# Two weight slots loaded and split ahead on GpSimd, and the last two rows' scale moved there

## What is computed

```
merged = sigmoid(mg_a + b_gate[0]) * y_a + sigmoid(mg_b + b_gate[1]) * y_b
sub = merged @ w_out                         # (512 x 2048) by (2048 x 2048)
z = ALPHA * x + sub
out = (z - mean(z)) * rsqrt(var(z) + eps) * ln_g + ln_b     # per row
```

## Time and profile before

| what | us |
|---|---|
| median of three runs | 1378.58 |
| the profiled execution | 1378.59 |
| its span | 1376.8 |
| TensorE busy | 1359.2 (99%) |
| TensorE's weight loads busy | 1153.8 (84%) |
| GpSimd busy | 683.3 (50%) |
| ScalarE busy | 575.9 (42%) |
| vector engine busy | 482.2 (35%) |
| TensorE's last product starts | 1365.86 |

### The profile page before, as it was taken

The page is one execution under the profiler, slowest core; times in us unless marked ns, Lnnn a source line. Parts: engine busy times, 40 slices in busy tenths (PEclk is TensorE's granted clock), DMA queues, the critical chain, the costliest instruction groups (busy, mean ns, idle before and its releaser), DMA issues.

```text
span 1376.8 us, 19878 instructions
## 1 busy us (share of the span) xinstructions
PE 1359.2 (99%) x6488; PEld 1153.8 (84%) x6488; DVE 482.2 (35%) x844; ACT 575.9 (42%) x972; POOL 683.3 (50%) x514
## 2 busy tenths in 40 slices
PE   9999999999999999999999999999999999999996
PEld 7888888888988988898898888888888888888885
DVE  7776675652030222204111011010101202297687
ACT  5455464543471374356247222222222222445443
POOL 7543443455455555546454556464555636422216
PEclk9999999999999999999999999999999999999999
DMA  9432241445374254427434344663536446377674
GB/s 282 112 123 77 76 137 55 129 119 127 88 165 149 82 120 130 127 83 173 139 111 143 88 152 117 143 141 101 170 95 158 123 126 148 96 242 261 206 250 157
DMA packets 204991, 190.07 MB, mean 138 GB/s; under 512 B 16529, under 2 KB 178577, under 8 KB 204945
## 3 DMA queue, kind: packets, MB, share of 16 engines
q1 hardware_dynamic: 191344, 151.74, 37.3%
q0 software_dynamic: 13600, 37.75, 11.1%
HBM read 185.23 MB, written 41.94 MB: 165 GB/s over the span
## 4 chain that ended last, share of the span: by engine, by line
PE 68%; issue 16%; POOL 11%; DMA 2%; ACT 1%; DVE 1%; SPq 0%; POOLq 0%; ACTq 0%
PE acc L1517 61%; POOL w_lo L574 6%; POOL w_lo L573 5%; PE ps_scores L1517 2%; PE ps_out L1517 1%; PE ps_turn L1517 1%; PE ps_out L1607 1%; DMA raw<-w_in 1%; DMA first_raw<-w_in 1%; DMA raw<-w_out 0%; PE ps_turn L1579 0%; PE ps_scores L1544 0%; PE ps_scores L1541 0%; DVE z L1377 0%; ACT w_hi L627 0%
## 5 line engine op out<-in xcount | busy, mean ns | idle before, releaser
L573 POOL TENSOR_TENSOR w_lo<-raw,w_hi 128x512 fp32r<-128x512 f32 x238 | 317.5, 1334 | 676.2 <-ACT w_hi L627 567.7
L1517 PE MATMUL acc<-x_hi,w_hi 128*128 128x512 f32 x1216 | 478.0, 393 | 0.0
L1517 PE MATMUL acc<-x_hi,w_lo 128*128 128x512 f32 x1216 | 474.2, 390 | 0.0
L1517 PE MATMUL acc<-x_lo,w_hi 128*128 128x512 f32 x1216 | 474.0, 390 | 0.0
L627 ACT ACTIVATE w_hi<-raw 128x1024 fp32r<-128x1024 f32 x224 | 234.3, 1057 | 342.8 <-PE acc L1517 333.1
L574 POOL TENSOR_TENSOR w_lo<-raw,w_hi 128x512 fp32r<-128x512 f32 x238 | 328.7, 1381 | 0.0
L1517 PEld LDWEIGHTS acc<-x_hi,w_lo 128*128 128x128 f32 x1216 | 228.3, 188 | 48.1
L1517 PEld LDWEIGHTS acc<-x_lo,w_hi 128*128 128x128 f32 x1216 | 228.5, 188 | 44.1
L1517 PEld LDWEIGHTS acc<-x_hi,w_hi 128*128 128x128 f32 x1216 | 228.5, 188 | 44.1 <-POOL w_lo L574 0.2
L1242 DVE TENSOR_TENSOR part_a<-acc,part_a 128x512 f32<-128x512 f32 x16 | 11.1, 691 | 321.7 <-PE acc L1517 321.5
L1517 PE MATMUL acc<-w_hi,x_lo 128*128 128x384 f32 x256 | 85.6, 334 | 0.0
(11 more groups left out here) (277 smaller groups left out, 1631.2 us busy)
## 6 DMA issues: line engine op xcount, KB each, us to landing
raw<-w_in SPq DMA_DIRECT2D x384, 128.0 KB, 2.3
q_left<-w_out POOLq DMA_DIRECT2D x12, 2048.0 KB, 13.9
raw<-w_in SPq DMA_DIRECT2D x256, 96.0 KB, 2.6
raw<-q_left SPq DMA_DIRECT2D x32, 512.0 KB, 4.6
raw<-w_in SPq DMA_DIRECT2D x64, 192.0 KB, 2.9
raw<-w_pa SPq DMA_DIRECT2D x64, 128.0 KB, 6.2
raw<-w_out SPq DMA_DIRECT2D x16, 512.0 KB, 4.3
first_raw<-xT SPq DMA_DIRECT2D x8, 512.0 KB, 9.2
```

The source lines that it names most:

```text
L573: nc.gpsimd.tensor_tensor(dst[:, left], src[:, left], hi[:, left].bitcast(F32), ALU.subtract)
L1517: ins = nc.tensor.matmul(into[:, 0:cols], s, m, start=start and k == 0, stop=stop and k == n - 1)
```

## The change

`RING_JOBS` is 54. SyncE's ring ends there, and the raw tiles of jobs 54 and 55 are loaded to `more_raw`, memory of its own in the place of the low parts of the left sums, right behind its turns 43 and 44. ScalarE copies their high parts in its turns 45 and 46, behind the high parts of jobs 47 and 48, and GpSimd makes both low parts behind that of job 46, each by one subtraction of 1024 columns. The vector engine no longer makes them.

For the row tiles n = 2 and 3 the vector engine makes only the reciprocal of `row_scale`; the four tensor_scalar steps are made by GpSimd, ahead of its two passes for that tile. The vector engine's first near pass no longer waits for them, its second does. GpSimd's columns of the layer norm start at 1024, 1024 and 1536 instead of 1024, 896 and 1408.

```diff
--- before.py
+++ after.py
@@ -168,7 +168,8 @@
 LN_ROWS = (2, 3, 0, 1)
 END_HIGH = (17, 19, 21, 23, 25, 27)
 TOGETHER = 6
-LN_SPLIT = (D, 1024, 896, 1408)
+RING_JOBS = O_JOBS - (TOGETHER - RING)
+LN_SPLIT = (D, 1024, 1024, 1536)
 LN_FIRST = 1024
 
 
@@ -249,6 +250,7 @@
         z = at("z", og_at, [P, NR, D])
         g_row, b_row = at("g_row", x_at, [P, D]), at("b_row", x_at + 4 * D, [P, D])
         more_hi, more_lo = (at(n, x_at + 8 * D + 8192 * k, [P, TOGETHER - RING, SLOT], F32R) for k, n in enumerate(("more_hi", "more_lo")))
+        more_raw = at("more_raw", x_at + 4 * KT * SEQ, [P, TOGETHER - RING, SLOT])
         end_hi = at("end_hi", og_at + 4 * NR * D, [P, 2, HALF, 2 * P], F32R)
 
         shared_at = top[0]
@@ -348,6 +350,8 @@
         u_ready, v_ready, z_scaled, z_ready, row_ready = (sem("u_ready"), sem("v_ready"), sem("z_scaled"), sem("z_ready"),
                                                           sem("row_ready"))
         far_in = sem("far_in")
+        more_in = [sem(f"more_in{n}") for n in range(TOGETHER - RING)]
+        more_hi_done, more_lo_done = sem("more_hi_done"), sem("more_lo_done")
         var_ready, root_ready = sem("var_ready"), sem("root_ready")
         stats_ready, ln_step, centred, scaled, finished = (sem("stats_ready"), sem("ln_step"), sem("centred"),
                                                            sem("scaled"), sem("finished"))
@@ -385,7 +389,9 @@
 
         def low_ready(engine, q):
 
-            if q < 0:
+            if q >= RING_JOBS:
+                engine.wait_ge(more_lo_done, q - RING_JOBS + 1)
+            elif q < 0:
                 engine.wait_ge(lo_done, JOB_O + q + (1 - PRO_JOBS + 4))
             elif q in POOL_LOW:
                 engine.wait_ge(lo_done, JOB_O + (1 - PRO_JOBS + 4) + POOL_LOW.index(q))
@@ -507,7 +513,7 @@
 
             def jobs_o():
                 sp.wait_ge(summed, 16 * SUMS)
-                for q in range(O_JOBS):
+                for q in range(RING_JOBS):
                     low_ready(sp, q - RING)
                     dst = raw[:, q % RING, :]
                     if QUARTER_JOB[0] <= q < LAST_JOB[0]:
@@ -521,6 +527,8 @@
                         sp.wait_ge(full[7], fills_o(7) + 2)
                     if q in (37, 39, 41, 43):
                         load_row((q - 37) // 2)
+                    if q in (43, 44):
+                        sp.dma_start(more_raw[:, q - 43, :], load_o(RING_JOBS + q - 43)).then_inc(more_in[q - 43], 16)
 
             def load_x(piece):
 
@@ -605,9 +613,28 @@
             for q in POOL_LOW:
                 hi, lo = slot_o(q)
                 low(lo, raw[:, q % RING, :], hi, JOB_O + q)
+                if q == 46:
+                    for n in range(TOGETHER - RING):
+                        pool.wait_ge(more_hi_done, n + 1)
+                        nc.gpsimd.tensor_tensor(more_lo[:, n, :], more_raw[:, n, :], more_hi[:, n, :].bitcast(F32),
+                                                ALU.subtract).then_inc(more_lo_done, 1)
             pool.wait_ge(row_in, 32)
             pool.wait_ge(far_in, 32)
+            def row_scale(n):
+                var, inv, cor = variance[:, n:n + 1], rstd[:, n:n + 1], correction[:, n:n + 1]
+                pool.wait_ge(ln_step, 6 * n + 2)
+                nc.gpsimd.tensor_scalar(cor, inv, inv, var, ALU.mult, ALU.mult).then_inc(ln_step, 1)
+                pool.wait_ge(ln_step, 6 * n + 3)
+                nc.gpsimd.tensor_scalar(cor, cor, -0.5, 1.5, ALU.mult, ALU.add).then_inc(ln_step, 1)
+                pool.wait_ge(ln_step, 6 * n + 4)
+                nc.gpsimd.tensor_scalar(inv, inv, cor, None, ALU.mult).then_inc(ln_step, 1)
+                pool.wait_ge(ln_step, 6 * n + 5)
+                nc.gpsimd.tensor_scalar(shift[:, n:n + 1], meanvar[:, n, 0:1], inv, -1.0,
+                                        ALU.mult, ALU.mult).then_inc(ln_step, 1)
+
             for n, r in enumerate(LN_ROWS[1:]):
+                if n:
+                    row_scale(n + 1)
                 columns, width = z[:, r, LN_SPLIT[n + 1]:D], slice(LN_SPLIT[n + 1], D)
                 pool.wait_ge(centred, n + 1)
                 nc.gpsimd.tensor_tensor(columns, columns, g_row[:, width], ALU.mult).then_inc(finished, 1)
@@ -852,11 +879,13 @@
 
                 s, (hi, _) = q % RING, slot_o(q)
                 act.wait_ge(raw_in[s], 16 * JOB_O - 16 * LOADS * PRO_JOBS // RING + 16 * (q // RING + 1))
-                if q < O_JOBS - (TOGETHER - RING):
-                    act.wait_ge(slot_used, JOB_O + (q - 2 * RING - RING + 1))
-                elif q == O_JOBS - (TOGETHER - RING):
-                    act.wait_ge(full[7], fills_o(7) + 2)
+                act.wait_ge(slot_used, JOB_O + (q - 2 * RING - RING + 1))
                 nc.scalar.activation(hi, raw[:, s, :], ACT.Copy).then_inc(hi_done, 1)
+
+            def more_high(n):
+                act.wait_ge(more_in[n], 16)
+                act.wait_ge(full[7], fills_o(7) + 2)
+                nc.scalar.activation(more_hi[:, n, :], more_raw[:, n, :], ACT.Copy).then_inc(more_hi_done, 1)
 
             def pair_high(n):
 
@@ -895,8 +924,10 @@
 
             def jobs_o():
                 for q in range(O_JOBS):
-                    if q + AHEAD < O_JOBS:
+                    if q + AHEAD < RING_JOBS:
                         high_o(q + AHEAD)
+                    if q in (45, 46):
+                        more_high(q - 45)
                     if q == 1:
                         sums_high(2)
                     if q == 3:
@@ -1385,10 +1416,13 @@
                 dve.wait_ge(ln_step, 6 * n + 1)
                 nc.vector.tensor_scalar(variance[:, n:n + 1], meanvar[:, n, 1:2], EPS, None, ALU.add).then_inc(var_ready, 1)
 
+            def row_inverse(n):
+                dve.wait_ge(root_ready, n + 1)
+                nc.vector.reciprocal(rstd[:, n:n + 1], root[:, n:n + 1]).then_inc(ln_step, 1)
+
             def row_scale(n):
+                row_inverse(n)
                 var, inv, cor = variance[:, n:n + 1], rstd[:, n:n + 1], correction[:, n:n + 1]
-                dve.wait_ge(root_ready, n + 1)
-                nc.vector.reciprocal(inv, root[:, n:n + 1]).then_inc(ln_step, 1)
 
                 dve.wait_ge(ln_step, 6 * n + 2)
                 nc.vector.tensor_scalar(cor, inv, inv, var, ALU.mult, ALU.mult).then_inc(ln_step, 1)
@@ -1405,12 +1439,13 @@
                 inv, mean = rstd[:, n:n + 1], meanvar[:, n, 0:1]
                 if n == 0:
                     dve.wait_ge(rows_copied, 1)
-                dve.wait_ge(ln_step, 6 * n + 6)
+                dve.wait_ge(ln_step, 6 * n + (6 if n < 2 else 1))
                 width = min(LN_SPLIT[n], LN_FIRST)
                 whole, left, right = z[:, r, 0:width], z[:, r, 0:SEQ], z[:, r, SEQ:width]
                 nc.vector.scalar_tensor_tensor(whole, whole, mean, ps_scores[:, 0:width],
                                                ALU.subtract, ALU.mult).then_inc(scaled, 1)
                 dve.wait_ge(scaled, 3 * n + 1)
+                dve.wait_ge(ln_step, 6 * n + 6)
                 nc.vector.scalar_tensor_tensor(left, left, inv, ps_turn[:], ALU.mult, ALU.add).then_inc(scaled, 1)
                 nc.vector.scalar_tensor_tensor(right, right, inv, ps_out[:, 0:width - SEQ],
                                                ALU.mult, ALU.add).then_inc(scaled, 1)
@@ -1486,7 +1521,7 @@
                     add_product(P2, 1, r)
                     add_product(P3, 1, r)
                     row_moments(n, r, 14 + 2 * r)
-                    row_scale(n)
+                    row_inverse(n)
                     row_near(n, r)
 
             iter_a(0, False)
```

## The result

The changed kernel takes **1381.2 us** (median of ten runs, 1380.27 to 1383.31); the kernel before, run beside it, 1378.34 us (ten runs, 1378.0 to 1378.58). The ratio is 1.0023, with a 95% interval of 1.0015 to 1.0031: 2.9 us slower, just over the 0.2% named as what can be told. The forecast was 1380.7 us. The profiled execution took 1382.08 us, with a span of 1380.3 us; the span before was 1376.8, so the traces are 3.5 us apart.

A forecast was written before the change was run, and what follows sets the result against it. TensorE, busy 1359.2 of 1376.8 us, was taken to bound the kernel, so only its stalls or the tail count. -1.7 (stall) + 3.9 (holds) - 0.1 (tail) = +2.1 us gave 1380.7 us, range 1376.6 to 1382.3.

The forecast's parts named there:

- The stall of slot 55: TensorE's wait near the last slots goes once slots 54 and 55 are ready early: 4.42 to 2.7 us, -1.7 us.
- The holds: GpSimd's two subtractions and the vector engine's SBUF passes before unit 0's additions to z delay each other: +3.9 us.
- Rival A: Nothing holds at the vector engine's passes: they don't meet GpSimd's, or there is enough slack; 1376.8 us, chance 0.13.
- Rival B: The vector engine keeps its turn over back-to-back passes, GpSimd enters only at an idle 0.31 us; 1378.8 us, chance 0.09.
- The rule that spoke against the change: Two-SBUF-input VectorE instructions and reading GpSimd ones exclude each other; the change costs up to two whole passes (4.5 us).
- The loads: Two added 512 KB loads on SyncE's queue around load 44, costed at nothing; if cover were gone, 6.1 us less ScalarE's waits.
- Rival D: Loads 54 and 55 land after 1332.9, ScalarE stands at their copies; slower by some 4 us, chance 0.03.
- The tail: After the last reciprocal, the last two rows' scale moves to GpSimd: 5.18 to 5.0 us, -0.1 in the sum.
- C: Length of the four small scale steps on GpSimd: taken as 1.4 us, 0.33 a step, between 0.6 and 2.2.
- Rival C: GpSimd's small scale steps are dear, slow side from 1.7 us for the four; 1382.3 us at 2.2; chance 0.15.
- The estimate from the price of reads: GpSimd's scale steps at 85 ns a read: eleven operands 0.9 us, four steps 1.4 to 2, sum up to 1.2 longer.
- slower by over 0.2%: Sign for the whole kernel: slower by more than 2.8 us, chance 0.18; within 0.2% had 0.80, faster 0.02.

The follow-up runs named there:

- x4: The changed kernel with its two added loads issued behind loads 41 and 42 instead of 43 and 44; 1380.52 us.
- x3: The changed kernel with GpSimd's two subtractions for slots 54 and 55 made memsets to zero, which read nothing; 1376.47 us.
- x7: The changed kernel with only the second of GpSimd's two subtractions made a memset to zero; 1379.01 us.
- x8: The changed kernel with both subtractions made memsets and the two added loads issued behind loads 41 and 42; 1376.29 us.
- x1: The changed kernel with the layer norm's scale back on the vector engine and the old column split; 1381.19 us.
- x5: The changed kernel with loads behind 41 and 42, high parts in ScalarE's turns 40 and 41, GpSimd's subtractions ahead of slot 44; 1375.91 us.

## Why the prediction was right, and where it was not

The forecast was 1380.7, the result 1381.2, slower by a mechanism that the prediction named, with its two passes. Point by point:

- **The stall of slot 55:** forecast -1.7, measured -1.69 (4.42 to 2.73 us).
- **The holds:** forecast +3.9, and x4 measures +3.93. In the change itself they fell on the low part of 47 and one far pass, not on both far passes, since the vector engine came later than GpSimd to the first meeting; each still cost 1.9 to 2.2 us. Rival A (nothing holds) falls by x3: with the reads gone, 1376.47 us, where it put 1376.8. Rival B (one turn only) falls by the two held instructions in a row, and x7 shows what one would be, with the late load in it: 1379.01 us, where it put 1378.8. The turns are as read from the earlier trace rows: the one that stood waiting went next each time.
- **The rule that spoke against the change:** the rows of before and after agree with what the Trainium skill says in "SBUF — State Buffer", section "Who interferes with whom": two-input VectorE work and a reading GpSimd instruction exclude each other. The same section says that a GpSimd instruction that only writes doesn't contend, and x3 agrees (a memset of 0.95 us beside an unchanged 1.22).
- **The loads, the term that was mis-sized:** costed at nothing, measured 1.1 us at the vector engine's low part of 45 and 0.8 at the additions (4.76 against 3.93; 0.5 by x3 against x8). The step that failed was to judge the cover of every slot by ScalarE's 1.66 us waits for TensorE, and not to ask how much slower the neighbours' loads would become. Slot 45 has no such wait: between the high parts of 44 and 45 ScalarE also copies g_row, loads a table and takes the root, and works without a gap. Its cover was the 4.0 us by which its load landed early, and the load became 5.1 us slower (4.3 to 9.41). The bound that the prediction gave for a lost cover, 6.1 us less the waits, was wide enough for the 1.1 us.
- **Rival D** falls: the two added loads land 5.6 and 7.3 us behind their issue, by 1325, and ScalarE's copy of the first starts at 1333.25 without a wait for it. A load did come late, but it was the neighbour's of slot 45.
- **The clock, a term that was missing:** +0.56. TensorE's stall was in the sum, a slower clock behind it was not.
- **The tail:** forecast -0.1 with C = 1.4; the chain has -0.14 with C = 1.50, 0.27 us a step on average and 0.1 between. The other 0.41 us behind the last pass were not in the sum. Rival C falls: it needed C = 1.7. The estimate from the price of reads in "GPSIMD Engine Reference" of the Trainium skill ("Performance pitfalls for Q7 kernels"), C of 1.4 to 2, has the measured 1.50 near its low end. It counted eleven operands, but the four steps read eight, which at that price would be an estimated 0.7 us instead of 0.9; no run here shows the price of a read by itself.

The forecast's sum from the stage is +2.1, the trace's +3.1: 0.8 for the loads and 0.6 for the clock too little, 0.4 too much for the tail's end. The errors partly cancel in the total, so that its nearness says less than the experiments on the single terms do. The prediction gave "slower by over 0.2%" 0.18, and the ratio is 1.0023, with an interval that begins below that bound.

What stays open: why runs of the change and of x1 spread over 3 to 4 us where those of the kernel before stay within 2.3, but for one of 63. The slow clock is in both traces taken of them, and the slowest run of x1 (1384.13 us) has a mean clock of 0.995 against 0.996 to 0.998 of the others, but only one execution of each has a trace.

## What to carry to other kernels

Before moving work to an idle engine, list what the other engine on the same memory runs in that stretch: an idle GpSimd above a busy vector engine is not free time, and each meeting of two reading instructions costs up to the length of GpSimd's (here 1.9 to 2.2 us of 2.4). Moved to a stretch where the vector engine reads PSUM, the same work made the additions 0.4 us late instead of 4.8 (x5). And take the cover of a load from its own landing and the one instruction that needs it, not from the usual wait in the loop, and expect the loads behind an added one to become slower; where the step that is moved makes TensorE stand, look at its granted clock afterwards.

## What the runs showed of the hardware that was not expected

- GpSimd's memset of 128x1024 float32 takes 0.95 us and holds no two-input instruction of the vector engine (x3); its subtraction of the same tile takes 2.41 us and holds them.
- A stall of 2.67 us and the thin work after it were followed by some 3.4 us at TensorE's 1.2 GHz level (granted clock 0.57 over 1347 to 1351 us), in the change and in x1; a stall of 1.83 us in x4 was not. What led the clock to fall was not tried by itself. The price was 0.56 us, less than the slow products by themselves, for TensorE was then waiting on the vector engine at each step.
- The load of slot 45 took 9.41 us as the last of four issued within 2.6 us; in the kernel before, without the two added ones, the same load took 4.3.
